# A hybrid encoder layer on one core: the input projection as three fp32r products, all u tiles in the first stage

## The reference, cut to what matters

```python
x = layer_norm(concat(x_prompt, x_sample))         # 1088 tokens x 1024, fp32
p = x @ w_in                                       # 1024 -> 2048, fp32
u, gb, gc, v = split(p, 4)                         # 512 columns each
y_ssm = s5_ssm(u, ...)                             # 32 groups of 16 channels, a diagonal complex scan
g = gelu(y_ssm)
y_ssm = g * sigmoid(g @ w_glu + b_glu)
y_conv = gb * causal_conv3(gc * v)                 # width 3, along the tokens
mixed = concat(rms_norm(y_ssm, beta_ssm), rms_norm(y_conv, beta_conv))
x = layer_norm(alpha * x + mixed @ w_out)
x = layer_norm(alpha * x + moe(x))                 # 64 experts, top 6 of 4 expert groups, one shared expert
```

## Times and profile before

| what | value |
| --- | --- |
| median of 3 runs | 1520.47 us (1513.76 to 1523.84) |
| the profiled execution, its own time | 1520.43 us |
| its span | 1518.7 us |
| mean granted TensorE clock | 0.945 |
| PE busy | 1309.8 us, 86% of the span |
| DVE, ACT, POOL busy | 1076.9, 863.3, 771.4 us |
| trunk, mixing, gate, output projection, experts, final | 86.5, 278.0, 54.5, 239.0, 809.0, 51.7 us |

### The profile page before, as it was taken

How to read it: one execution, slowest core, us unless ns; L and a number is a source line. 1 busy time by engine, 2 the same in 40 slices (tenths; PEclk the granted TensorE clock), 3 DMA queues, 4 the chain that set the end, 5 groups by cost and what they waited for, 6 DMA issues and landing times. The chain is left out here.

```text
span 1518.7 us, 23302 instructions
## 1 busy us (share of the span) xinstructions
PE 1309.8 (86%) x6003; PEld 1029.5 (68%) x6003; DVE 1076.9 (71%) x1414; ACT 863.3 (57%) x1008; POOL 771.4 (51%) x652
## 2 busy tenths in 40 slices
PE   4898997895799979949989999999999999999920
PEld 3556665573578757747878787877878787787810
DVE  5634743540758886548988888888888888898828
ACT  6410110103735453238878787787877878788735
POOL 1156653303421553324767776766767566677720
PEclk9999999998989989979999999999999999999975
DMA  9152463606432343345989999999999999999647
GB/s 282 70 130 42 73 43 72 74 12 100 153 113 105 97 155 152 115 165 218 310 295 335 326 330 352 333 345 306 346 333 324 343 332 325 323 319 360 179 139 279
DMA packets 113058, 330.43 MB, mean 218 GB/s; under 512 B 30657, under 2 KB 61377, under 8 KB 88433
## 3 DMA queue, kind: packets, MB, share of 16 engines
q1 hardware_dynamic: 87824, 276.05, 53.5%
q0 software_dynamic: 24752, 53.73, 14.2%
q10 hardware_dynamic: 432, 0.07, 0.0%
HBM read 287.06 MB, written 68.91 MB: 234 GB/s over the span
## 5 line engine op out<-in xcount | busy, mean ns | idle before, releaser
L2101 DVE TENSOR_TENSOR moe_up_l<-rt_raw_up,moe_up_h 128x2048 fp32r<-128x2048 f32 x154 | 352.6, 2291 | 107.0 <-ACT moe_up_h L1918 106.5
L1918 ACT ACTIVATE moe_up_h<-rt_raw_up 128x2048 fp32r x154 | 294.1, 1912 | 123.6 <-DMA rt_raw_up<-in_w_up_dram 89.7
L2009 POOL DMA_INDIRECT acc<-moe_y,moe_idx_s x77 | 243.3, 3160 | 65.4 <-POOL moe_idx_s L2006 43.5
L2040 PE MATMUL moe_p_gu<-moe_up_h,moe_x_h 128*128 128x512 f32 x616 | 244.6, 397 | 3.2 <-DVE moe_x_l L2110 2.0
L2040 PE MATMUL moe_p_gu<-moe_up_l,moe_x_h 128*128 128x512 f32 x616 | 243.8, 396 | 0.0
L2040 PE MATMUL moe_p_gu<-moe_up_h,moe_x_l 128*128 128x512 f32 x616 | 243.8, 396 | 0.0
L2000 POOL DMA_INDIRECT moe_xg<-tok,moe_idx_g x79 | 168.8, 2137 | 66.9 <-POOL moe_idx_g L1997 64.0
L737 PE MATMUL mix_proj<-co_hT,co_win 128*128 128x384 f32 (+1 forms) x624 | 194.8, 474 | 2.3 <-PEq L110 2.3
L2122 DVE TENSOR_TENSOR moe_dn_l<-rt_raw_dn,moe_dn_h 128x2048 fp32r<-128x2048 f32 x77 | 175.9, 2285 | 4.8 <-ACT moe_dn_h L1964 4.7
L737 PEld LDWEIGHTS mix_proj<-co_hT,co_win 128*128 128x128 f32 x624 | 119.3, 192 | 74.4 <-issue 5.7
L2052 PE MATMUL moe_p_dn<-moe_dn_h,moe_hid_h 128*128 128x512 f32 x308 | 132.0, 429 | 35.5 <-DVE moe_dn_l L2122 34.2
(11 more groups left out here) (419 smaller groups left out, 2260.2 us busy)
## 6 DMA issues: line engine op xcount, KB each, us to landing
rt_raw_up<-in_w_gate_dram SPq DMA_DIRECT2D x64, 1024.0 KB, 9.1
rt_raw_up<-in_w_up_dram SPq DMA_DIRECT2D x64, 1024.0 KB, 12.9
rt_raw_dn<-in_w_down_dram SPq DMA_DIRECT2D x64, 1024.0 KB, 7.9
acc<-proj_ax SPq DMA_DIRECT2D x18, 512.0 KB, 2.7
final_x<-acc SPq DMA_DIRECT2D x18, 512.0 KB, 12.9
co_win<-in_w_in_dram SPq DMA_DIRECT2D x16, 512.0 KB, 4.3
resid<-trunk_x SPq DMA_DIRECT2D x9, 512.0 KB
proj_res<-resid SPq DMA_DIRECT2D x9, 512.0 KB, 3.3
```

The source lines that it names most:

```text
L1918: act.activation(up_h[:, par, half, :, :], raw_up[:, bass.ds(slot, 1), half, :, :].rearrange("p a k n -> p (a k) n"), ACT.Copy).then_inc(u ...
L2009: pool.indirect_dma_start(out=io.acc[par], in_=y[:, par, :], in_offset=None, out_offset=bass.IndirectOffsetOnAxis(ap=idx_s[:, par:par + 1] ...
L2040: mm = pe.matmul(p_gu[:, par, :].rearrange("p (a n) -> p a n", a=2), x, w, start=(i == 0), stop=(i == len(terms) - 1))
L2101: low = tt(up_l[:, par, half, :, :], raw_up[:, bass.ds(slot, 1), half, :, :].rearrange("p a k n -> p (a k) n"), up_h[:, par, half, :, :].b ...
```

## The change

The weights and the transposed tokens of the input projection are kept as two fp32r parts each, high (the value rounded by ACT's copy) and low (the difference, by DVE). A chunk is now 24 products instead of 8: high by high, high weights by low tokens, low weights by high tokens. The fp32 copies go: tokens are split straight from the transposes' PSUM buffer, which has three slots and is released by DVE's subtraction; weights come into two raw slots (three before) and are split into a ring of three. In the trunk ACT takes the statistics of all nine token tiles. All four u tiles are computed there (u 3 as the last three chunks, whose SBUF space is that of u 0, when this is written); SP writes them to `ud` and, at the end of the stage, waits until these writes have landed. `MIX_ORDER` begins with v 0 instead of u 3, and gc 0 stands ahead of S 0, no longer between S 0 and Y 0. Two weight tiles ahead of each use, ACT and DVE split the next one.

The mixing stage leaves its results in HBM: the load of `yd` back into `gT`, and SP's wait ahead of it, are gone; the convolution's result goes into `gb` and, after each gb tile, SP waits for it and writes it to a new HBM buffer `yc`. The gate stage begins with loads: four of `gT` (544 KB each), `w_glu`, and one of `ycT` (2176 KB), all ahead of the small rows and of the raw pieces on SP's queue. GELU runs in 12 passes, one per chunk and tile, and PE's first products of a chunk wait for the passes that they read. POOL's squares wait for `ycT`. In the output projection ACT computes only minus the mean beside the root; DVE makes the norm, gain and offset in two passes, as in `affine`; POOL adds no offset, and `put` is no longer behind that.

```diff
-IN_RING = 3
+IN_RING = 2
+SPLIT_RING = 3
...
-U_FIRST = 3
+U_FIRST = 4
+U_WIDE = 3
 COLUMN = {"u": 0, "gb": KH, "gc": 2 * KH, "v": 3 * KH}
-MIX_ORDER = [("u", 3), ("T", 0), ("v", 0), ("S", 0), ("gc", 0), ("Y", 0),
+MIX_ORDER = [("v", 0), ("T", 0), ("gc", 0), ("S", 0), ("Y", 0),
...
+        u_parts = [(ch, c) for ch in range(len(TOK_CHUNKS)) for c in range(U_WIDE)]
+        u_parts += [(ch, U_WIDE) for ch in range(len(TOK_CHUNKS))]
...
             def weight(i):
                 kind, c = IN_TILES[i]
+                if i >= IN_RING:
+                    sp.wait_ge(co.s_wl, i - IN_RING + 1)
...
             for c in range(U_FIRST):
 
-                sp.wait_ge(s_u, 2 * U_FIRST + c + 1)
-                weight(U_FIRST + c)
-                sp.wait_ge(s_uact, 2 * U_FIRST + c + 1)
-                sp.dma_start(io.ud[c * P:(c + 1) * P, :], keep.gT[:, c, 0:N_TOK]).then_inc(co.s_uout[c], 16)
+                sp.wait_ge(s_uact, last_part[c] + 1)
+                sp.dma_start(io.ud[c * P:(c + 1) * P, :], ut[:, c % U_WIDE, :]).then_inc(co.s_uout[c], 16)
+                if c == U_WIDE - 1:
+                    weight(5)
...
+            for c in range(U_FIRST):
+                sp.wait_ge(co.s_uout[c], 16)
...
+            def high(i):
+
+                act.wait_ge(co.s_w[i % IN_RING], 16 * (i // IN_RING + 1))
+                if i >= SPLIT_RING:
+                    act.wait_ge(s_u, last_part[i - SPLIT_RING] + 1)
+                act.activation(co.win_h[:, i % SPLIT_RING, :, :], co.win[:, i % IN_RING, :, :], ACT.Copy).then_inc(co.s_wh, 1)
...
-                    if n >= 2:
-                        pe.wait_ge(s_ev, n - 1)
+                    if n >= 3:
+                        pe.wait_ge(s_low, n - 2)
...
+                terms = [(a[:, c % SPLIT_RING, k, :], b[:, k, lo:lo + ln]) for k in range(KD)
+                         for a, b in ((co.win_h, co.hT_h), (co.win_h, co.hT_l), (co.win_l, co.hT_h))]
+                for j, (a, b) in enumerate(terms):
...
+            def low(i):
+                w = P if i < N_TILES - 1 else LAST_ROWS
+                for half in range(2):
+                    n = 2 * i + half
+                    at = (slice(None), slice(4 * half, 4 * half + 4), slice(i * P, i * P + w))
+                    v.wait_ge(s_ev, n + 1)
+                    tt(co.hT_l[at], pst[:, n % 3, :, 0:w], co.hT_h[at].bitcast(F32), ALU.subtract).then_inc(s_low, 1)
+
+            def low_w(i):
+                v.wait_ge(co.s_wh, i + 1)
+                tt(co.win_l[:, i % SPLIT_RING, :, :], co.win[:, i % IN_RING, :, :],
+                   co.win_h[:, i % SPLIT_RING, :, :].bitcast(F32), ALU.subtract).then_inc(co.s_wl, 1)
...
             affine(1)
+            low_w(0)
             affine(2)
+            low(0)
+            low_w(1)
+            low(1)
...
+            low_w(2)
             affine(3)
             affine(4)
...
             affine(5)
+            low(3)
+            low(4)
...
             affine(8)
+            for i in (6, 7, 8):
+                low(i)
...
+            low_w(3)
+            low_w(4)
...
+                if kind == "gb":
+
+                    sp.wait_ge(s_conv, c + 1)
+                    sp.dma_start(io.yc[c * P:(c + 1) * P, :], gb[:, :]).then_inc(s_ycout, 16)
...
-                    sp.wait_ge(s_uout[c], 16)
...
-                    sp.wait_ge(s_yout, 16 * T * (c + 1))
-                    sp.dma_start(gT[:, c, :], io.yd[c * P:(c + 1) * P, :]).then_inc(s_yin, 16)
...
+            sp.wait_ge(s_yout, 16 * T * KH)
+            sp.wait_ge(s_ycout, 16 * KH)
...
+        passes = [(ch, c) for c in range(KH) for ch in (0, 1)] + [(2, c) for c in range(KH)]
...
+            for c in range(KH):
+                sp.dma_start(gT[:, c, 0:N_TOK], io.yd[c * P:(c + 1) * P, :]).then_inc(s_y[c], 16)
             sp.dma_start(w_glu[:, :, :], io.w_glu[0].rearrange("(k p) n -> p k n", p=P)).then_inc(s_wg, 16)
+            sp.dma_start(ycT[:, :, 0:N_TOK], io.yc.rearrange("(c p) n -> p c n", p=P)).then_inc(s_yc, 16)
...
+            for ch, c in passes:
+                lo, ln = TOK_CHUNKS[ch]
+                steps = slice(lo // T, (lo + ln) // T)
+                act.wait_ge(s_y[c], 16)
+                act.activation(gn[:, c, lo:lo + ln].rearrange("p (k s) -> p s k", s=T),
+                               gT[:, c, 0:N_TOK].rearrange("p (s k) -> p s k", s=T)[:, :, steps],
...
+            pool.wait_ge(s_yc, 16)
...
+                    if mo == 0:
+                        pe.wait_ge(s_gelu, passes.index((ch, k)) + 1)
...
-                act.wait_ge(s_rstd, i + 1)
-                act.activation(x[:, i % 2, :], x[:, i % 2, :], ACT.Identity, bias=rs[:, 1:2],
-                               scale=rs[:, 0:1]).then_inc(s_nm, 1)
+                act.wait_ge(s_zd, i + 1)
+                act.activation(rs[:, 1:2], mv[:, 0:1], ACT.Copy, scale=-1.0).then_inc(s_neg, 1)
...
-            def offset(i):
-                pool.wait_ge(s_gain, i + 1)
-                pool.tensor_tensor(x[:, i % 2, :], x[:, i % 2, :], lnb[:, :], ALU.add).then_inc(s_x, 1)
...
+                v.wait_ge(s_neg, i + 1)
                 link(v.reciprocal(rs[:, 0:1], rs[:, 0:1]))
-                link(stt(out=rs[:, 1:2], in0=mv[:, 0:1], scalar=-1.0, in1=rs[:, 0:1], op0=ALU.mult, op1=ALU.mult),
-                     s_rstd)
-
-            def gain(i):
-                v.wait_ge(s_nm, i + 1)
                 if i == 0:
                     v.wait_ge(s_ln, 32)
-                tt(x[:, i % 2, :], x[:, i % 2, :], lng[:, :], ALU.mult).then_inc(s_gain, 1)
+                link(stt(out=x[:, i % 2, :], in0=x[:, i % 2, :], scalar=rs[:, 1:2], in1=lng[:, :], op0=ALU.add,
+                         op1=ALU.mult))
+                stt(out=x[:, i % 2, :], in0=x[:, i % 2, :], scalar=rs[:, 0:1], in1=lnb[:, :], op0=ALU.mult,
+                    op1=ALU.add).then_inc(s_x, 1)
```

More of the change, by code:

```diff
@@ L118, in trunk_stage @@
         lng, lnb = m.sb("lng", [P, D]), m.sb("lnb", [P, D])
-        spare = m.sb("spare", [P, D])
-        stats = m.sb("stats", [P, 2, 6])
-        mv = m.sb("mv", [P, N_TILES, 2])
+        spare = keep.small[:, :]
+        ut = m.sb("ut", [P, U_WIDE, N_TOK])
         sums, neg = m.sb("sums", [P, N_TILES]), m.sb("neg", [P, N_TILES])
@@ L291, in _ @@
             u_out(5)
+            high(3)
             for k, dst in enumerate((co.cs, co.csw)):
                 act.wait_ge(s_part, 2 + k)
-                act.activation(dst[:, :], pso[:, 1 + k, :], ACT.Copy)
-            for n in (6, 7, 8):
+                act.activation(dst[:, :], pso[:, k, :], ACT.Copy)
+            u_out(6)
+            high(4)
+            for n in range(7, len(u_parts)):
                 u_out(n)
@@ L367, in _ @@
             pe.wait_ge(s_c, 64)
+            pe.wait_ge(s_parc, 1)
             for v, src in enumerate((crow, crow_sw)):
                 for k in range(KH):
-                    tr = pe.transpose(pso[:, 1 + v, k * P:(k + 1) * P], src[:, k, :], keep.ident[:, :])
+                    tr = pe.transpose(pso[:, v, k * P:(k + 1) * P], src[:, k, :], keep.ident[:, :])
                 tr.then_inc(s_part, 1)
-            for n in (6, 7, 8):
+            for n in range(6, len(u_parts)):
                 u_part(n)
@@ L461, in _ @@
             link(tt(pi[:, :, 1], mag, sin, ALU.mult))
+            low(5)
             for n in (1, 2, 4):
@@ L539, in mixing_stage @@
         swap = m.sb("swap", [P, P])
-        fo = m.sb("fo", [GROUPS, 2, P])
+        fo = keep.small[0:GROUPS, 0:2 * P].rearrange("p (a b) -> p a b", a=2)
         proj = m.ps("proj", [P, 3, 512])
@@ L952, in gate_stage @@
         s_wg, s_small = m.sem("wg"), m.sem("small")
+        s_y, s_yc = [m.sem(f"y{c}") for c in range(KH)], m.sem("yc")
         s_raw = [m.sem(f"raw{k}") for k in range(3)]
@@ L1391, in _ @@
             for i in range(N_TILES):
-                offset(i)
-                if i >= 3:
-                    put(i - 3)
-            for i in range(N_TILES - 3, N_TILES):
                 put(i)
@@ L1742, in _ @@
                     norm(i - 1)
-                    gain(i - 1)
                 total(i, 0)
```

233 lines of the change are left out of this document (113 added, 120 removed).

## The result

| | before | after |
| --- | --- | --- |
| median of 20 runs each, on the same chips | 1522.72 us (1513.76 to 1528.07) | 1513.08 us (1507.9 to 1520.35) |
| ratio, 95% interval | | 0.9944 [0.9931, 0.9957] |
| span of the profiled execution | 1518.7 | 1510.2 |
| trunk | 86.5 | 102.1 (+15.6; forecast +22) |
| mixing | 278.0 | 248.95 (-29.05; forecast -17.5) |

The change makes the kernel 0.6% faster: the range held it, the direction did not. The forecast was +11.5 us. The medians differ by -9.6, the profiled executions by -8.5: -6.6 in the four stages and -1.9 where the text is the same. Mixing is 11.5 us off, the trunk 6.4.

The account below looks back on a forecast made before the run. It took PE to bound mixing, chains the trunk and gate stage, DVE the output projection; +22 - 17.5 + 9 - 2 = +11.5 us on 1520.4 gave 1532 us, range 1503 to 1550.

Parts of the forecast that it names:

- S 2 and S 3 waited 14.7 in all for u: Mixing: SP's queue loses a wait and load but still sends reads behind writes, so these waits shrink by 3 us.
- u 3 and 12 cheaper tiles: Mixing: u 3 leaves (14.7 us) and 12 tiles save 2.2 each (26.3), together -41 us.
- S 0: Mixing: PE arrives before POOL's first tables end and waits 8 us, +4 over before.
- Y 0: Mixing: nothing covers DVE's rotation and scan any more, so PE waits, about +8 us.
- S 1: Mixing: PE waits up to 12 us for POOL's second tables, taken as +9.
- end, clock, T: Mixing: last write of `yc` ends the stage, +1.5 us; slower clock after two more idle stretches, +4.
- rival 2: Saving is kept: products cost only their columns, trunk subtractions fall in DVE's waits; 1502 to 1510 us, chance 0.18.
- rival 3: Products cost 0.233 us at any width, a tile 16.8, so the change doesn't cheapen them; 1580 us, chance 0.05.
- The trunk: Trunk stage: +22 us from products (+6), delays of the three groups (+3, +5, +5) and the end (+3).
- The gate stage: Gate stage: +9 us, +8 from loads delaying the first gated product and 1 for POOL's squares beside DVE.
- rival 1: Port contention: POOL's squares and tables slow beside DVE's two-input passes; gate +18, S 1's wait +16; 1548 us, chance 0.30.
- The output projection: Output projection: two DVE passes of 1.285 us per tile replace idle and gain; -2 us.

Follow-up runs that it names:

- b_rows: Kernel before, cached columns transposed by PE and sent as rows of 512 B instead of 4 B elements; mixing 260.5 us, whole 1502.79 us, ratio 0.9872.
- b_cols: Kernel before, only the cached columns moved on POOL's queue, quarters 0 and 1 ahead of the next quarters' tables; mixing 292.0 us, whole 1538.79 us, once.
- a_ywait: Changed kernel, SP's wait for a quarter's writes to yd put back ahead of the next reads of u; mixing 251.3 us, whole 1518.78 us, once.
- a_nolow: Changed kernel without DVE's subtractions for the tokens' low parts, the second product reading the high ones; trunk 96.0 us (whole time not comparable).
- a_nosq: Changed kernel without POOL's squares of the convolution's result, a memset in their place; gate stage 56.6 us (whole time not comparable).
- a_rows: Changed kernel, cached columns written as rows instead of 4 B elements; mixing 249.4 us, whole 1509.91 us, ratio 0.9909 to the kernel before.

## Why the prediction was wrong

**The step that failed: "S 2 and S 3 waited 14.7 in all for u ... still sends the reads behind the writes: -3."** I read the wait as SP's queue. The writes that the queue waited for were slow because POOL's columns were in flight beside them: b_rows sends these as rows and the wait is gone, b_cols puts them beside the writes of three quarters and S 1 waits too, a_ywait restores the queue's wait and finds 1.7 us. In the changed kernel the tables of quarter 2 end 9 us later in the stage (132.5 against 123.5), so the columns leave behind Y's writes, and the stall is gone by a shift in time that nothing in the diff aims at. PE gets 14.7 back and gives 6.8 for `mix_kf` in their place: -7.9 instead of -3. The trace of the kernel before could have told me: 17.7 us from the writes to the read with columns beside them in quarter 1, 5.7 without in quarter 0.

**The other terms of mixing.** Of the 11.5 us, S 2 and S 3 are 4.9; the product's price is more, 6.5.

| term | forecast | measured |
| --- | --- | --- |
| u 3 and 12 cheaper tiles | -41 | -47.5 (14.7 + 12 x 2.73) |
| S 0 | +4 | +6.0 (10.20 - 4.17) |
| Y 0 | +8 | +8.2 |
| S 1 | +9 | +9.0 (10.83 against 1.86) |
| S 2, S 3 | -3 | -7.9 |
| end, clock, T | +5.5 | +3.1 |

That makes -29.1, the whole of the -29.05. In the last row the end gave +0.4 for +1.5 (PE's last product to the next stage, 6.1 us against 5.7), the slower clock, 0.91 for 0.96, +1.6 for +4 (PE's tiles as they ran fell from 193.7 to 147.3 us, 1.1 less than by their price, and its other products took 0.5 longer), and T's waits +1.1, which I had not counted. The forecast's +5.5 was 2.4 too much. The price was mis-sized from both sides: I carried the 0.02 us that a product of 512 columns costs beyond its columns to 384 and got 0.18; it was 0.1734, 0.0134 beyond 0.16. And a tile before cost 14.6 rather than 14.5: the 48 records of 14.79 us were a whole tile, 16 products of 384 columns and 8 of 320, which I read as 24 of 384. A tile saves 2.73, not 2.2. So rival 2's "products cost only their columns" is half true, and rival 3 is out.

The Trainium skill ("FP8 and Floating Point Precision", TensorE Precision Notes) states four passes for fp32; if an fp32r product is one, three of them cost three quarters, 10.9 a tile by estimate. The trace gives 11.84 of 14.6, 0.81, between that rule and my value.

**The trunk, +15.6 for +22.** The second group was to start at 53 and started at 49.03; the third's further +5 did not come. Of the 6.4 us, 2.4 are the price again (4 x 11.84 against 3 x 14.6, +3.6 for +6) and 0.7 the end (+2.3 for +3). The rest, 3.3, lies in the delays: I had 13, and 15.6 less the other two leaves 9.7. Of the 13, 9.3 were the tokens' subtractions (1.3 + 4.0 + 4.0); a_nolow prices them at 6.1. I take it that I added the subtractions of each group as if PE had been on the chain all along, though cheaper products had just made it idle ahead of each group, so that part of each delay fell in that idle time. What I placed right is u 3: the 9.2 us behind 69.17 are its chunks, 11.84, less what the cheaper products of that group save.

**The gate stage, +8.65 for +9: right by two errors.** Loads delay the first gated product by 2.3 instead of 8: PE has `w_glu` at 10.9 and ends its first chunk at 16.3, and ACT goes on at once to the sigmoid's table and, at 17.7, the sigmoid. The small row that it needs, forecast at 20, had landed at 16.6 (354.13 and 13.5 us to landing). POOL's squares beside DVE, which I put at 1, cost 6.6 (a_nosq). This is rival 1's mechanism: squares took 27.8 us, the "27 instead of 21" of that rival, and PE's sums had to wait; at 21.3 us, by my estimate, the squares would have ended at 389.0, ahead of PE's coming at 391.8. I had let PE wait "on a path that has some 7 to spare"; the wait of 3.77 and the low clock behind it, 4.7, used that up. The stage did not go to the rival's +18, which was for squares of 30 us and the longer chain of loads.

The Trainium skill ("SBUF — State Buffer", SBUF: two separate sides) states that DVE with two SBUF inputs and GpSimd share a port pair, which one of them holds for a whole instruction. The trace fits: 1.84 against 1.28 us on DVE, 1.69 against 0.82 on POOL, and both short again when the other is absent.

**The output projection** went as forecast: no idle between the passes, -1.8.

**The forecast without the accident.** Against a kernel before that has no slow columns the three stages cost +13.5 and the projection -1.8, about +11.7 in the profiled executions, and +7.1 in the times (a_rows against b_rows). So the direction turned on a stall of the kernel before, which I took for a part of its design: -9.6 with it, +7.1 without. That +11.7 comes near my +11.5 is luck: mine counts 3 us of the stall as gone, and the trunk was 6 too high and mixing 6 too low by the measure of b_rows. Nor does the stall alone mend my sum. With S 2 and S 3 put right (4.9) it gives +6.6, with the price put right in mixing and trunk (8.9) +2.6, and only with both -2.3.

## What to carry to other kernels

Before a wait for a transfer is priced by its queue, look at what else is in the DMA engines at that moment, on any queue, and how small its pieces are; then take away that neighbour alone in the old kernel. A gain that comes with a change may belong to a coincidence in time that a small edit elsewhere repairs without it. And where products get cheaper, their cover gets shorter: the order of the tiles should be written anew for the waits that show (here another 19 us of mixing).
